# Routing the expert gates of a two-layer encoder through a device-memory matrix instead of one-hot matmuls

## The reference, cut to what matters

```python
def peer(h, w_query, sub_keys, expert_down, expert_up):
    q = (x @ w_query).reshape(T, PEER_HEADS, 2, D_HALF)              # 8 heads, two halves
    s = jnp.einsum('thcd,hckd->thck', q, sub_keys)                   # 128 keys a half
    s1, i1 = lax.top_k(s[:, :, 0], PEER_TOPK)                        # 16 best of each half
    s2, i2 = lax.top_k(s[:, :, 1], PEER_TOPK)
    cand = s1[..., :, None] + s2[..., None, :]                       # 256 sums a head
    top_s, pos = lax.top_k(cand, PEER_TOPK)                          # the 16 best of them
    idx = take(i1 * N_KEYS + i2, pos)                                # which of 16384 experts
    gate = softmax(top_s)
    a = gelu(x . expert_down[idx])                                   # a number per chosen expert
    y = sum(a * gate * expert_up[idx])
```

## Time and profile before

| | |
|---|---|
| median of 3 runs | 2118.96 us (2115.63 to 2122.14) |
| the profiled execution, from its first to its last instruction | 2118.7 us |
| PE busy | 2072.3 us, 98% |
| DVE busy | 1575.6 us, 74% |
| ACT busy | 936.8 us, 44% |
| POOL busy | 25.9 us, 1% |
| DMA | 352.62 MB, 166 GB/s on the mean |
| TensorE clock granted | 0.993 of full speed |

### The profile page before, as it was taken

The page is one execution under the profiler, slowest core; times in us unless marked ns, Lnnn a source line. Parts: engine busy times, 40 slices in busy tenths (PEclk is TensorE's granted clock), DMA queues, the critical chain, the costliest instruction groups (busy, mean ns, idle before and its releaser), DMA issues.

```text
span 2118.7 us, 46598 instructions
## 1 busy us (share of the span) xinstructions
PE 2072.3 (98%) x15150; PEld 1877.0 (89%) x15150; DVE 1575.6 (74%) x3577; ACT 936.8 (44%) x1456; POOL 25.9 (1%) x49
## 2 busy tenths in 40 slices
PE   7999999999999999999999999999999999999998
PEld 6789999999988888887889989999999988888886
DVE  5858999767678887666578758999767678887665
ACT  5644455333333334555444444455333333334453
POOL 1000000000000000000000000000000000000000
PEclk9999999999999999999999999999999999999999
DMA  5344555444444446775545545555444444445554
GB/s 211 138 141 169 188 172 177 149 144 143 139 140 148 148 148 200 240 243 198 198 143 174 176 151 169 186 171 179 149 140 147 139 137 146 147 147 176 195 191 158
DMA packets 95678, 352.62 MB, mean 166 GB/s; under 512 B 10763, under 2 KB 10795, under 8 KB 95116
## 3 DMA queue, kind: packets, MB, share of 16 engines
q1 hardware_dynamic: 92252, 335.66, 47.9%
q0 software_dynamic: 3376, 16.31, 2.0%
HBM read 348.75 MB, written 3.18 MB: 166 GB/s over the span
## 4 chain that ended last, share of the span: by engine, by line
PE 94%; DVE 2%; DMA 1%; ACT 1%; issue 1%; POOL 0%; DVEq 0%; SPq 0%; ACTq 0%; POOLq 0%
PE psum L1104 28%; PE psum L1105 27%; PE psum L1106 27%; PE psum L1335 9%; DMA big<-bias_rows 1%; PE psum L1285 1%; PE psum L1262 1%; DVE big L683 0%; DVE w_lo L644 0%; PE psum L1189 0%; PE psum L1178 0%; PE psum L1215 0%; PE psum L1142 0%; DMA raw<-in_attn_units 0%; ACT w_hi L386 0%
## 5 line engine op out<-in xcount | busy, mean ns | idle before, releaser
L644 DVE TENSOR_TENSOR w_lo<-raw,w_hi 128x1024 fp32r<-128x1024 f32 x636 | 773.2, 1221 | 84.9 <-ACT w_hi L386 82.0
L1104 PE MATMUL psum<-x_hi,w_hi 128*128 128x256 f32 x2576 | 745.1, 289 | 6.9 <-DVE x_lo L670 3.0
L1105 PE MATMUL psum<-x_lo,w_hi 128*128 128x256 f32 x2576 | 730.5, 284 | 0.0
L1106 PE MATMUL psum<-x_hi,w_lo 128*128 128x256 f32 x2576 | 729.9, 283 | 0.0
L386 ACT CAST w_hi<-raw 128x1024 fp32r<-128x1024 f32 x636 | 661.8, 1046 | 12.5 <-PE psum L1106 8.8
L1104 PEld LDWEIGHTS psum<-x_hi,w_hi 128*128 128x128 f32 x2576 | 497.6, 193 | 10.7 <-issue 4.2
L1105 PEld LDWEIGHTS psum<-x_lo,w_hi 128*128 128x128 f32 x2576 | 496.0, 193 | 0.9
L1106 PEld LDWEIGHTS psum<-x_hi,w_lo 128*128 128x128 f32 x2576 | 495.4, 192 | 0.0
L1104 PE MATMUL psum<-w_hi,l_hi 128*128 128x512 f32 x1152 | 463.5, 402 | 1.0 <-DVE l_lo L742 1.0
L1106 PE MATMUL psum<-w_hi,l_lo 128*128 128x512 f32 x1152 | 449.4, 390 | 0.0
L1105 PE MATMUL psum<-w_lo,l_hi 128*128 128x512 f32 x1152 | 448.7, 389 | 0.0
(11 more groups left out here) (142 smaller groups left out, 1014.0 us busy)
## 6 DMA issues: line engine op xcount, KB each, us to landing
raw<-in_down SPq DMA_DIRECT2D x256, 512.0 KB, 3.3
raw<-in_up SPq DMA_DIRECT2D x256, 512.0 KB, 3.6
raw<-in_sg_units SPq DMA_DIRECT2D x72, 512.0 KB, 4.1
raw<-in_query SPq DMA_DIRECT2D x32, 512.0 KB, 3.3
raw<-in_attn_units SPq DMA_DIRECT2D x20, 512.0 KB, 4.6
big<-bias_rows POOLq DMA_DIRECT2D x1, 3072.0 KB, 17.4
big<-in_sub_keys POOLq DMA_DIRECT2D x2, 1024.0 KB, 6.0
h_kept<-big POOLq DMA_DIRECT2D x2, 1024.0 KB, 4.2
```

The costliest lines, as they stand in the source:

```text
L644: dve.tensor_tensor(w_lo[n % SPLIT][:, :], raw[n % RAW][:, :], w_hi[n % SPLIT][:, :].bitcast(F32), ALU.subtract).then_inc(lo_done, 1)
L1104: pe.matmul(out_ap, hi_s, hi_m, start=start, stop=False)
L1105: pe.matmul(out_ap, hi_s, lo_m, start=False, stop=False)
L1106: return pe.matmul(out_ap, lo_s, hi_m, start=False, stop=stop)
```

## The change

The bf16 one-hots, their matmuls, `turn_picks`, `take_picks` and the half-by-half gating go. In their place:

- A matrix `gates` in device memory for each layer, 128 units x 128 partitions x 256 tokens of fp32 (16.8 MB). GpSimd fills it with zeros by 32 transfers of four units each, in layer 0 beside attention units 9 to 20 and query units, in layer 1 beside the gated mixer's units.
- The items are taken head by head, both token tiles of a head after each other (a pair). After each pair DVE computes an address a choice and ACT the exponentials of the pair (two of 128 x 16, each of which also sums), so there are 8 softmax steps a layer and not 2.
- `scatter`: for each pair GpSimd issues 32 indirect transfers, one for each of 2 token tiles x 16 choices. One takes 128 addresses and 128 gates (one a partition, that is one a token) and adds each gate to its place in the matrix. It waits for the gates of the pair, and for all transfers of the pair before to have landed. That makes 256 a layer.
- SP loads a 128 x 256 tile of the matrix (`g_t`, 128 KB, four buffers) behind each up unit's `raw`. The first four wait until all 256 transfers of the layer have landed; later ones wait for their buffer.
- DVE multiplies each tile of `acts` with its `g_t` two up units ahead; all down units and all up units now run without gate matmuls.

```diff
@@ buffers, semaphores @@
+    gates = [nc.dram_tensor(f"gates{n}", (NK, P, T), F32, kind="Internal").ap() for n in range(DEPTH)]
+        g_t = [sb(f"g_t{s}", [P, T]) for s in range(G_TILES)]
@@ SP @@
-                stream(u["up"], NK,
-                       lambda i, c: up_units[layer][:, bass.ds((i * GROUP + c) * D, D)])
+                def up_unit(c, i):
+                    load(u["up"] + c, up_units[layer][:, bass.ds((i * GROUP + c) * D, D)], i)
+                    if isinstance(i, int):
+                        sp.wait_ge(added[layer], 16 * ITEMS * TOPK)
+                    else:
+                        sp.wait_ge(gated_up, i * GROUP + (layer * NK + c - G_TILES + 1))
+                    sp.dma_start(g_t[c][:, :], gates[layer][bass.ds(i * GROUP + c, 1)].rearrange("o p t -> (o p) t")
+                                 ).then_inc(g_landed[c], 16)
@@ GpSimd @@
+            def clear(layer, chunks, at):
+                for q in chunks:
+                    pool.wait_ge(used, at(q))
+                    pool.dma_start(gates[layer][ZERO_UNITS * q:ZERO_UNITS * q + ZERO_UNITS].rearrange("i p t -> p i t"),
+                                   zeros[:, :].rearrange("p (o t) -> p o t", o=1).broadcast_to([P, ZERO_UNITS, T])
+                                   ).then_inc(zeroed, 16)
+            def scatter(layer):
+                pool.wait_ge(zeroed, 16 * (layer + 1) * (NK // ZERO_UNITS))
+                flat = bass.AP(gates[layer].tensor, 0, [[1, NK * P * T], [1, 1]])
+                for i in range(PH):
+                    pool.wait_ge(gate_done, PH * layer + i + 1)
+                    if i:
+                        pool.wait_ge(added[layer], 16 * PAIR * i)
+                    for t in range(TT):
+                        for k in range(TOPK):
+                            at = PAIR * i + TOPK * t + k
+                            pool.indirect_dma_start(flat, bass.IndirectOffsetOnAxis(address[:, at:at + 1], 0),
+                                                    vals[:, TT * i + t, k:k + 1], None, element_offset=P * t,
+                                                    compute_op=ALU.add).then_inc(added[layer], 16)
+                if layer == 0:
+                    clear(0, range(24), lambda q: 9 + 11 * q // 24)
+                else:
+                    clear(1, range(8), lambda q: at + 2 + 2 * q)
+                    clear(1, range(8, 32), lambda q: at + SG_V_UNITS + 4 + q)
@@ ACT @@
-                def exponentials(t):
-                    v = vals[:, PH * t:PH * t + PH, :]
-                    act.wait_ge(shifted, TT * layer + t + 1)
-                    act.activation(v, v, ACT.Exp).then_inc(exp_done, 1)
+                def exponentials(k, i=0):
+                    act.wait_ge(shifted, i + (PH * layer + k + 1))
+                    for t in range(TT):
+                        v = vals[:, bass.ds(i * TT + (TT * k + t), 1), :].rearrange("p o k -> p (o k)")
+                        ins = act.activation(v, v, ACT.Exp, bias=least[:, t:t + 1], accum_out=sums[:, t:t + 1])
+                    ins.then_inc(exp_done, 1)
                     act.preload_act_table(ACT.Gelu_apprx_tanh)
...
+                        evict(n, i, TT * GROUP)
+                        if k == 0 and c == 0 and not first:
+                            exponentials(-1, i)
@@ DVE @@
+                def gates_of_pair(k, i=0):
+                    dve.wait_ge(d, own.value())
+                    step(dve.scalar_tensor_tensor(out=expert[:, :], in0=chosen[:, 1, :], scalar=float(NK), in1=chosen[:, 0, :],
+                                                  op0=ALU.mult, op1=ALU.add))
+                    dve.tensor_scalar(address[:, bass.ds(i * PAIR + PAIR * k, PAIR)], expert[:, :], float(T), token[:, 0:1],
+                                      ALU.mult, ALU.add)
+                    dve.wait_ge(exp_done, i + (PH * layer + k + 1))
+                    step(dve.reciprocal(sums[:, :], sums[:, :]))
+                    v = vals[:, bass.ds(i * TT + TT * k, TT), :]
+                    dve.tensor_tensor(v, v, sums[:, :].rearrange("p (m o) -> p m o", o=1).broadcast_to([P, TT, TOPK]), ALU.mult
+                                      ).then_inc(gate_done, 1)
...
+                def gate(n, i=0):
+                    dve.wait_ge(g_landed[n % G_TILES], i * 16 + 16 * (layer * NK // G_TILES + n // G_TILES + 1))
+                    a = acts[:, bass.ds(i * GROUP + n, 1), :]
+                    dve.tensor_tensor(a, a, g_t[n % G_TILES][:, :].rearrange("p (o t) -> p o t", o=1), ALU.mult
+                                      ).then_inc(gated_up, 1)
@@ PE: gates(), turn_picks() and their calls go @@
-                    for r in range(4):
-                        for q in range(PARTS):
-                            ins = pe.matmul(pg[c % 2][:, r * HALF:r * HALF + HALF], one1[c % 2][:, :, r],
-                                            gated2[c % 2][:, q, :, r], start=q == 0, stop=q == PARTS - 1)
-                    ins.then_inc(g_done, 1)
```

More of the change, by code:

```diff
@@ L101, in build @@
         iota = sb("iota", [P, P])
[L102 to L107, removed]
+        zeros = sb("zeros", [P, T])
+        token = sb("token", [P, 1])
+        vals = sb("vals", [P, ITEMS, TOPK])
+        address = sb("address", [P, ITEMS * TOPK], U32)
+        expert = sb("expert", [P, PAIR])
+        least = sb("least", [P, TT])
+        sums = sb("sums", [P, TT])
+        g_t = [sb(f"g_t{s}", [P, T]) for s in range(G_TILES)]
         gains = sb("gains", [P, 2 * DEPTH, KD])
@@ L347, in _ @@
                 pool.dma_start(h_kept, h.rearrange("p t d -> p (t d)")).then_inc(h_stored, 16)
+                if layer == 0:
+                    clear(0, range(24, 32), lambda q: ATTN_UNITS + q - 23)
+                scatter(layer)
                 up = unit0[layer]["up"]
@@ L1042, in _ @@
-                take_picks(1)
-                with dve.Fori(2, HALF // GROUP - 1) as i:
-                    own.loop(i, 4, 2)
-                    for c in range(GROUP):
-                        first_half(c, i, (0, c + 1, i))
-                    own.end(HALF // GROUP - 1)
-                i = HALF // GROUP - 1
-                for c in range(GROUP - 1):
-                    first_half(c, i, (0, c + 1, i))
-                first_half(GROUP - 1, i, (1, 0, 0))
-                gate(0, GROUP - 1, i)
+                items(1, True, True)
@@ new lines, in _ @@
+                with dve.Fori(1, PH - 1) as i:
+                    own.loop(i, PAIR_STEPS, 1)
+                    items(0, True, True, range(GROUP), i, -1)
+                    items(1, True, True, range(GROUP), i)
+                    own.end(PH - 1)
+                items(0, True, True, range(GROUP), PH - 1, -1)
+                items(1, False, True, range(GROUP + 1), PH - 1)
+                for n in range(HALF + 1, HALF + 5):
+                    split_lo(u["down"] + n + AHEAD)
+                    if n == HALF + 3:
+                        gates_of_pair(PH - 1)
+                        dve.wait_ge(d, own.value())
+                        dve.sem_inc(items_done, 1)
@@ L1301, in _, with column @@
                     queries(i)
[L1302 to L1311 removed]
+                def column(c, i=0):
@@ L1369, in _ @@
[L1369 to L1373 removed]
+                    rows(u["up"] + c, c % 2, o0 + c + 1, c == 0, False)
+                with pe.Fori(1, NK // GROUP - 1) as i:
                     for c in range(GROUP):
```

319 lines of the change are left out of this document (95 added, 224 removed).

## The result

The changed kernel is slower: 2375.3 us median of 4 runs against 2117.3 before, a ratio of 1.1216 (1.12 to 1.1233). I had forecast 1925 us, and a range of 1900 to 2090.

A forecast was written before the change was run, and what follows sets the result against it. PE, 98% busy, was taken as the bound, with the scatter hidden: 2118.7 - 208 (gate matmuls) - 2 (transposes) + 11 (softmax steps) + 3.4 (down to up) = 1923, stated as 1925 us; range 1900 to 2090.

The forecast's parts named there:

- Gate matmuls out: Beside down and up units, 64 groups of 0.80 us and 64 of 0.827 leave PE's path: 208 us saved in all.
- Clears and gate tiles: Zeroing the matrix and loading gate tiles taken to cost nothing; clears at most 5 us in each layer.
- Between down and up: PE waits for a chain behind the last down unit's gelu: about 1.7 us a layer, 3.4 in all.
- Softmax steps: In the search stretch, 6 more steps a layer cost PE 0.88 us each: 11 us in all, at most 51.
- in another way: Sign of a wrong prediction: `w_lo` rows beyond 1.23 us or search units longer than 3.1 us.
- The threshold of the scatter: Under the down stage, 314 us for 256 issues: up to 1.23 us an issue stays hidden.
- The price of an issue: An indirect issue on POOL taken as 1.0 us, between direct issues of 0.52 and 1.21; scatter hidden.
- Rival 2: Each indirect issue waits out a 1.22 us DVE split, costing 1.76 us; PE starves, 2196 us, slower than before; chance 0.15.
- Rival 3: Each issue holds DVE 0.2 us, making DVE the bound of the search stretch: 90 us more, 2015 us; chance 0.06.

## Why the prediction was wrong

- **Gate matmuls out, 208 us.** Right: with the rest of the terms (-2, +11, +3.4) it gave 1923, and the run with 8 transfers a layer has 1940.
- **Clears and gate tiles, nothing.** Right: the spatial mixer's stretch is as long as before, and up units run at 2.72 us with the gate tiles loaded.
- **Between down and up, 1.7 us.** Right in size: 1.32.
- **Softmax steps, 11 us.** Mis-sized: 28 us. The term rested on one gap of 0.88 us, though the row of DVE said it had no slack for ACT's pauses. My sign of being wrong "in another way", search units over 3.1 us, did show (3.14), but not by the mechanism that I had tied to it.
- **The threshold of the scatter, 1.23 us an issue.** Right. From the runs it is 2.10 - 435 / 512 = 1.25 us.
- **The price of an issue, 1.0 us.** This is the step that failed. I took a value between two direct issues, 0.52 and 1.21 us, as though the dearest direct one were an upper end. Neither has an address list or an add. I also put the pause between two issues at nothing. The step measured 2.10: 1.54 for the issue, 0.30 to the next one, 0.21 on the mean for DVE's instructions and 0.05 of longer pauses. Even without the last two, 1.84 us is over the threshold by 0.6.
- **Rival 2.** Its side was right, and its mechanism was there: the issue waits out the rest of a DVE split that runs when it starts. But it was not what decided, so that it had the side right is in part luck. I gave it a full split for every issue on top of 0.54; in truth it is 0.21 us on the mean on top of 1.84. By my own formula, 1925 + 512 x (2.10 - 1.23) = 2370 us, against 2375 measured. That this is so close is luck too: the base was 15 us too low, and the excess over the threshold 10 too high (445 for 435).
- **Rival 3** falls as I gave it: in the changed kernel no issue holds DVE, `w_lo` is not lengthened beyond 1.27 us, and 8 or 128 issues a layer leave the search alike. DVE did become the bound of the search, by the softmax steps.
- What I gave 0.15 came true and lay outside my range. A cost that no row bounds from above, times 512, left more to the slow side than 0.16.

## What to carry to other kernels

Count the issues and ask what one may cost before the work behind them shows. Here that threshold, 1.23 us, lay within a factor of two of the nearest rows, and those rows lacked the operation: the unknown price was the forecast. The small transfers of this queue were paid by the issue far more than by the address (1.40 us for 64, 1.54 for 128), and moving only the part that fits under other work (here half of the tokens) beat both the kernel with all of it and the one with none. A load that waits for a late result also holds up every load behind it in its queue, here for 222 us.

## What the runs showed of the hardware

- An indirect, adding issue of 128 addresses holds POOL for 1.54 us and the next begins 0.30 later; with 64 addresses it is 1.40, and without the add 0.96. A direct one with the add takes 0.89 a step.
- It is held up by a DVE instruction with two inputs in SBUF that began before it, for what is left of that less some 0.12 us: up to 1.07 us beside a split of 1.22. One that begins 0.06 us later does not touch it, and DVE's row grows by 0.05 us at most. 25 issues that began in a reduction of 0.69 us with one input were not held, nor were direct issues in a split.
- Beside a split of one input that takes 0.69 us, the hold goes both ways: up to 0.52 us for an issue that begins in it, up to 0.62 for one in which it begins, and up to 0.33 for the split.
- 512 plain indirect writes of 4-byte pieces slowed everything beside them (66 GB/s of traffic in the down stage against 184 with adds); open why.
- In the hole the granted clock fell to 0.50. PE resumed at 777.22 us and had 0.50 until 781 us and 1.00 from there:

```profile
777.00:781.00 4.00, 3.78 (x9) 3.04 (x10) 2.31 (x5) 1.91 (x3) 0.00 (x0) 0.50 0.84 273
781.00:785.00 4.00, 4.00 (x19) 3.27 (x19) 1.90 (x3) 1.54 (x3) 0.00 (x0) 1.00 0.54 165
```
